# One table of expert slots in device memory, in place of counts and picks in every expert unit

## The chip, the cores and the metric

The kernel runs on one core of a Trainium2 chip. The metric is the time of one execution on the device in microseconds (us), the median of several runs. Engines are named TensorE (PE), VectorE (DVE), ScalarE (ACT), GpSimd (POOL) and SyncE (SP, which issues most transfers).

## The reference

A trunk of two layers over 256 tokens of width 1024, in float32. Layer 0 has neighbourhood attention, attention to a memory and a dense SwiGLU; layer 1 has gated linear attention, attention to the memory and the expert SwiGLU on which the change works:

```
logits = xf @ w_router                                   # 256 tokens, 8 experts
top_val, top_idx = lax.top_k(logits, 2)
weights = softmax(top_val)
y[token] = sum over its two experts e of
           weight * (silu(x @ w_gate[e]) * (x @ w_up[e])) @ w_down[e]
out = rms_norm(h + y)
```

Each expert has three matrices of 1024 x 3584, together 44 MB in float32; the eight experts have 352 MB, which are read once.

## The kernel before, in words

**Units.** The experts run as units of 128 slots: unit 0 to 7 are the experts' first 128 tokens, and up to three further units follow if an expert has more than 128 (with these inputs there are eight units). A unit has 42 weight blocks of 1 MB: for each of seven column blocks c of 512 hidden columns two gate halves, two up halves and two down halves. SyncE loads them some ten blocks ahead. ScalarE writes the rounded high part of a block (`w_hi`, L806), VectorE the rest (`w_lo`, L1399), and TensorE multiplies in three products (`mul3`, L1449: high by high, high by low, low by high). There are three places for cut blocks, so ScalarE may cut a block when TensorE has finished the one three before it.

**Order.** All engines have their program written out by hand; the unit is a loop on each of them (L793 ScalarE, L899 GpSimd, L1389 VectorE, L1944 TensorE), and semaphores tie them. TensorE goes gate(c), turning of the hidden values of c-1, up(c), down(c-1). VectorE cuts low parts in that order, and at the end of each c multiplies the gate's silu by the up product (L1418).

**Which rows a unit takes.** Before the units, VectorE finds the two largest logits of each token (L1313 to 1323) and TensorE sums one-hot masks to each token's rank within its expert (L1924 to 1928). `u_slot` holds for each token and unit the slot, and `u_wt` the weight. For a unit v `build_picks` makes a 0/1 matrix `pick` (token by slot) and puts the weight beside the token's number in `pick_w`:

```python
for t in range(TT):
    dve.tensor_scalar(pick[:, t, :], iota, u_slot[:, t, bass.ds(v, 1)], None,
                      ALU.is_equal).then_inc(pick_ready, 1)
dve.tensor_copy(pick_w[:, :, 1:2], u_wt[:, :, bass.ds(v, 1)]).then_inc(pick_ready, 1)
```

TensorE multiplies `pick` by `pick_w` (`count_picks`, L1985) and so gets, slot by slot, the token's number plus one and its weight. It does so twice in a unit u: behind the products of c = 3 with the picks of u, for the weights and the rows to which the outputs go (`slot_wt`, `row_to`, VectorE at c = 4, L1421 to 1431), and behind c = 5 with the picks of u+1, for the rows to gather (`row_of`, L1433 to 1435). GpSimd then gathers the next unit's rows from `xn_rows` by an indirect transfer (L903), and at a unit's end adds the weighted outputs to `h_rows` by another (L909). Unit 0's rows are not gathered so: TensorE picks them out of `xn` by 32 matmuls (`gather`, L1930).

**What stands ahead of the loop.** VectorE: masks, weights, ranks, picks of unit 0, the list of further units (`unit_i`, L1362 to 1382), the low parts of the gathered rows (`gather_low`, L1384), then the loop. GpSimd: the norm gain (L888), the copies of `xn` and `h` to device memory (L891, L894), then the loop. SyncE at the program's start: constants (L425), router weights (L426), norm gain (L427), then the remaining blocks of the first projection (L429).

Of the kernel before, what the change touches and what calls it, by code (L numbers as in the profile page):

```python
# [129 lines left out]
def shape_constants(np):  # L130

    i = np.arange(P)[:, None]
    j = np.arange(P)[None, :]
    same = (i // CH) == (j // CH)
    col = {}
    parts = []

    def put(name, a):
        full = np.zeros((P, a.shape[1]), np.float32)
        full[: a.shape[0]] = a  # L140
        col[name] = (sum(x.shape[1] for x in parts), a.shape[1])
# [12 lines left out]
    put("iota", np.broadcast_to(np.arange(P), (P, P)))  # L154
    put("token", 1.0 + np.arange(P)[:, None] + P * np.arange(TT)[None, :])
    put("spare", 1.0 + T + np.arange(P)[:, None])
# [16 lines left out]
def build(nc, col, tables, shifts, x, mem, gains, rpb, gate_aug, g_norm, router, mem_kv, even_in, even_out,  # L173
          even_gate, even_up, even_down, odd_in, odd_out, exp_gate, exp_up, exp_down, out):
    with ExitStack() as ctx:
# [29 lines left out]
        pick_w = sb("pick_w", [P, TT, 2])  # L205
        spare_row = sb("spare_row", [P, 1])
# [7 lines left out]
        xn_rows = nc.dram_tensor("xn_rows", (T, D), F32, kind="Internal").ap()  # L214
# [68 lines left out]
        u_slot = take(TT * UCOLS).rearrange("p (t u) -> p t u", t=TT)  # L283
        u_wt = take(TT * UCOLS).rearrange("p (t u) -> p t u", t=TT)
# [43 lines left out]
        r_logit, r_cand, r_one1, r_one2, r_rest, r_mask = (by_expert() for _ in range(6))  # L328
        r_m1, r_m2, r_idx, r_gap, r_gap_exp, r_w1, r_w2 = (take(TT) for _ in range(7))
        r_over, r_number = take(E), take(E)  # L330
# [6 lines left out]
        def STATE_PS(d, k):  # L337
# [47 lines left out]
        pick_ready, slots_counted, slot_part, gathered, gx_hi_ready, gx_lo_ready = (  # L385
            sem("pick_ready"), sem("slots_counted"), sem("slot_part"), sem("gathered"),
            sem("gx_hi_ready"), sem("gx_lo_ready"))
        y_half, y_ready, slot_known, h_kept, pool_turn2 = (
            sem("y_half"), sem("y_ready"), sem("slot_known"), sem("h_kept"), sem("pool_turn2"))
        pool_turn, rows_kept, rows_counted, rows_known, rows_in = (  # L390
            sem("pool_turn"), sem("rows_kept"), sem("rows_counted"), sem("rows_known"), sem("rows_in"))
# [7 lines left out]
        def _(sp):  # L399
# [26 lines left out]
            sp.dma_start(rt_sb[:], router.rearrange(kp, p=P)).then_inc(router_in, 16)  # L426
            sp.dma_start(gnb, g_norm.partition_broadcast(P)).then_inc(gnorm_in, 16)  # L427
# [422 lines left out]
        def _(pool):  # L850
# [38 lines left out]
            for t in range(TT):  # L889
                pool.wait_ge(xn_gained, 2 * (t + 1))  # L890
                nc.gpsimd.dma_start(xn_rows[P * t:P * (t + 1), :], xn[:, t, :]).then_inc(rows_kept, 16)  # L891
# [4 lines left out]
            nc.gpsimd.memset(mhalf[:, 5:6], 0.0).then_inc(pool_turn2, 1)  # L896
            pool.wait_ge(units_ready, 1)
            n_more = pool.value_load(unit_i[0:1, 0:1], min_val=0, max_val=3)
            with pool.Fori(0, n_more + E) as u:  # L899
                pool.wait_ge(rows_known, u + 1)  # L900
                pool.tensor_tensor(mhalf[:, 4:5], mhalf[:, 0:1], mhalf[:, 1:2], ALU.add).then_inc(pool_turn, 1)  # L901
                pool.wait_ge(rows_kept, 16 * TT)
# [12 lines left out]
        def _(dve):  # L915
# [408 lines left out]
            mark(dve.memset(u_slot, -1.0))  # L1324
            mark(dve.memset(u_wt, 0.0))
# [3 lines left out]
            mark(dve.reciprocal(r_w1, r_w1))  # L1329
            settle()  # L1330
            mark(dve.tensor_tensor(r_w2, r_gap_exp, r_w1, ALU.mult))
            settle()
            mark(dve.tensor_tensor(r_one1, r_one1, over_e(r_w1), ALU.mult))
            mark(dve.tensor_tensor(r_one2, r_one2, over_e(r_w2), ALU.mult))
            settle()
            mark(dve.tensor_tensor(u_wt[:, :, 0:E], r_one1, r_one2, ALU.add))
# [6 lines left out]
            mark(dve.tensor_scalar(u_slot[:, :, 0:E], r_cand, -1.0, None, ALU.add))  # L1343
            def build_picks(v):

                for t in range(TT):
                    dve.tensor_scalar(pick[:, t, :], iota, u_slot[:, t, bass.ds(v, 1)], None,
                                      ALU.is_equal).then_inc(pick_ready, 1)
                dve.tensor_copy(pick_w[:, :, 1:2], u_wt[:, :, bass.ds(v, 1)]).then_inc(pick_ready, 1)
# [7 lines left out]

            mark(dve.tensor_copy(pick_w[:, :, 0:1], const("token").unsqueeze(2)))
            settle()
            build_picks(0)  # L1360
# [22 lines left out]

            for b in range(2):  # L1384
                gather_low(0, b)
            dve.memset(ss[:, TT * 5:TT * 6, :], 0.0).then_inc(y_ready, 1)
            dve.wait_ge(units_ready, 1)
            n_more = dve.value_load(unit_i[0:1, 0:1], min_val=0, max_val=3)
            with dve.Fori(0, n_more + E) as u:  # L1389
# [20 lines left out]
                for c in range(NC):  # L1410
# [37 lines left out]
        def _(pe):  # L1448
# [481 lines left out]
            def gather(v, b):  # L1930
                pe.wait_ge(pick_ready, v * 3 + 2)
# [7 lines left out]
            for b in range(2):  # L1939
                gather(0, b)  # L1940
# [3 lines left out]
            with pe.Fori(0, n_more + E) as u:  # L1944
# [40 lines left out]
                def count_picks(at, ready, counted):  # L1985
                    pe.wait_ge(pick_ready, ready)
                    for t in range(TT):
                        ins = pe.matmul(ps[:, 7, at:at + 2], pick[:, t, :], pick_w[:, t, :],
                                        start=(t == 0), stop=(t == 1))
                    ins.then_inc(counted, 1)  # L1990

# [12 lines left out]
                for c in range(NC):  # L2004
# [61 lines left out]
```

## Time and profile before

| | |
|---|---|
| median of 3 runs | 1474.02 us (1472.86 to 1474.33) |
| span of the profiled execution | 1473.3 us (the profile shows no other time for it) |
| PE busy | 1418.6 us, 96% |
| PEld (weight loads) busy | 1188.8 us, 81% |
| DVE busy | 1157.7 us, 79% |
| ACT busy | 1000.6 us, 68% |
| POOL busy | 74.3 us, 5% |
| mean granted clock of TensorE | 0.989 of full speed |
| moved by transfers | 439.40 MB, mean 298 GB/s |

The profile is one execution. Busy shares are averages over all stages; the expert units fill the time from about 494 us to 1454 us. Matmuls are pipelined, so that the listed duration of one overlaps the next, and the distance from start to start is its pace. In a row of a timeline stand the start in us, the duration in us, engine, line, operation, what it writes and reads, and in brackets the idle time before it and what ended it.

### The profile page before, as it was taken

How to read it: one execution, taken by the hardware profiler on the slowest of the kernel's cores; microseconds unless marked ns; L12 is line 12 of the kernel's file. 1: busy time of each engine (PE TensorE's matmuls, PEld its weight loads, DVE VectorE, ACT ScalarE, POOL GpSimd, SP SyncE). 2: the span in 40 equal slices, each digit the busy share in tenths (PEclk: the TensorE clock that was granted, in tenths of full speed). 3: DMA queues.
4: the chain of work that ended last, by engine and by line, in shares of the span. 5: the costliest groups of instructions: out<-in, count | busy, mean ns of one | idle time of the engine just before them, and what ended most of it. 6: DMA issues, size and time to landing. Idle time of an engine off the chain costs nothing.

```text
span 1473.3 us, 19906 instructions
## 1 busy us (share of the span) xinstructions
PE 1418.6 (96%) x7273; PEld 1188.8 (81%) x7273; DVE 1157.7 (79%) x1040; ACT 1000.6 (68%) x949; POOL 74.3 (5%) x72
## 2 busy tenths in 40 slices
PE   6999999998998999999999999999999999999994
PEld 6996888887976788888888888888888888888883
DVE  5677655554674788898888888888889888888885
ACT  6455644445844577877787787787787778778775
POOL 0000000000011100100100100100010010010011
PEclk9999999999999899999999999999999999999997
DMA  9434465544445699999999999999999999999983
GB/s 314 167 115 143 147 203 194 183 135 130 157 158 198 221 380 357 358 404 374 371 379 388 361 374 397 357 367 404 368 347 404 373 369 383 387 359 376 397 304 128
DMA packets 201503, 439.40 MB, mean 298 GB/s; under 512 B 9135, under 2 KB 39411, under 8 KB 201460
## 3 DMA queue, kind: packets, MB, share of 16 engines
q1 hardware_dynamic: 198436, 427.82, 79.4%
q0 software_dynamic: 3024, 11.01, 2.9%
q8 instruction: 27, 0.44, 0.1%
q14 instruction: 16, 0.13, 0.0%
HBM read 430.93 MB, written 7.86 MB: 298 GB/s over the span
## 4 chain that ended last, share of the span: by engine, by line
issue 63%; PE 27%; POOL 3%; DVE 3%; ACT 2%; DMA 1%; POOLq 0%; SPq 0%; DVEq 0%; ACTq 0%
PE ps L1719 6%; PE ps L1451 5%; PE ps L1453 5%; PE ps L1452 5%; PE ps L1721 3%; POOL mhalf L901 1%; POOL arena L903 1%; POOL h_rows L909 1%; DVE w_lo L933 1%; ACT w_hi L516 1%; DMA raw<-mem_kv 1%; PE ps L1472 0%; PE ps L1575 0%; PE ps L1539 0%; PE ps L1902 0%
## 5 line engine op out<-in xcount | busy, mean ns | idle before, releaser
L1399 DVE TENSOR_TENSOR w_lo<-raw,w_hi 128x2048 fp32r<-128x2048 f32 (+1 forms) x224 | 442.2, 1986 | 67.0 <-ACT w_hi L806 65.4
L806 ACT ACTIVATE w_hi<-raw 128x2048 fp32r<-128x2048 f32 (+1 forms) x224 | 372.2, 1672 | 117.4 <-PE ps L1453 117.3
L1451 PE MATMUL ps<-w_hi,xt_both 128*128 128x512 f32 (+2 forms) x1048 | 408.8, 390 | 2.2 <-DVE xt_both L1284 1.5
L1453 PE MATMUL ps<-w_hi,xt_both 128*128 128x512 f32 (+2 forms) x1048 | 400.2, 382 | 0.0
L1452 PE MATMUL ps<-w_lo,xt_both 128*128 128x512 f32 (+2 forms) x1048 | 399.7, 381 | 0.0
L1399 DVE TENSOR_TENSOR w_lo<-arena,w_hi 128x2048 fp32r<-128x2048 f32 x144 | 294.1, 2052 | 20.4 <-ACT w_hi L806 19.7
L806 ACT ACTIVATE w_hi<-arena 128x2048 fp32r<-128x2048 f32 x144 | 248.9, 1728 | 77.1 <-PE ps L1453 77.1
L1451 PEld LDWEIGHTS ps<-w_hi,xt_both 128*128 128x128 f32 x1048 | 197.1, 188 | 44.6 <-DVE w_lo L1399 6.7
L1453 PEld LDWEIGHTS ps<-w_hi,xt_both 128*128 128x128 f32 x1048 | 196.9, 188 | 37.6
L1452 PEld LDWEIGHTS ps<-w_lo,xt_both 128*128 128x128 f32 x1048 | 197.3, 188 | 33.6
L1451 PE MATMUL ps<-w_hi,hT_hi 128*128 128x512 f32 x560 | 219.0, 391 | 0.0
L1453 PE MATMUL ps<-w_hi,hT_lo 128*128 128x512 f32 x560 | 218.3, 390 | 0.0
L1452 PE MATMUL ps<-w_lo,hT_hi 128*128 128x512 f32 x560 | 218.0, 389 | 0.0
L933 DVE TENSOR_TENSOR w_lo<-raw,w_hi 128x2048 fp32r<-128x2048 f32 (+2 forms) x69 | 149.4, 2171 | 68.6 <-ACT w_hi L516 68.5
L516 ACT ACTIVATE w_hi<-raw 128x2048 fp32r<-128x2048 f32 (+2 forms) x70 | 127.1, 1819 | 44.6 <-PE ps L1453 43.5
L1719 PE MATMUL ps<-xt_both,w_hi 128*128 128x512 f32 x352 | 124.9, 399 | 1.0 <-DVE xt_both L974 1.0
L1453 PEld LDWEIGHTS ps<-w_hi,hT_lo 128*128 128x128 f32 x560 | 105.1, 188 | 22.2
L1451 PEld LDWEIGHTS ps<-w_hi,hT_hi 128*128 128x128 f32 x560 | 105.2, 188 | 21.6
L1452 PEld LDWEIGHTS ps<-w_lo,hT_hi 128*128 128x128 f32 x560 | 105.2, 188 | 21.3
L1721 PE MATMUL ps<-xt_both,w_lo 128*128 128x256 f32 x352 | 98.8, 281 | 0.0
L1719 PEld LDWEIGHTS ps<-xt_both,w_hi 128*128 128x128 f32 x352 | 66.1, 188 | 17.7 <-issue 1.2
L1721 PEld LDWEIGHTS ps<-xt_both,w_lo 128*128 128x128 f32 x352 | 66.5, 189 | 0.4
(248 smaller groups left out, 1265.7 us busy)
## 6 DMA issues: line engine op xcount, KB each, us to landing
raw<-exp_gate SPq DMA_DIRECT2D x74, 1024.0 KB, 7.4
raw<-exp_up SPq DMA_DIRECT2D x49, 1024.0 KB, 7.5
arena<-exp_down SPq DMA_DIRECT2D x48, 1024.0 KB, 6.5
arena<-exp_up SPq DMA_DIRECT2D x40, 1024.0 KB, 8.0
raw<-exp_down SPq DMA_DIRECT2D x40, 1024.0 KB, 6.8
arena<-exp_gate SPq DMA_DIRECT2D x24, 1024.0 KB, 6.8
raw<-exp_up SPq DMA_DIRECT2D x32, 512.0 KB, 5.0
raw<-even_gate SPq DMA_DIRECT2D x11, 1024.0 KB, 5.4
```

The source lines that it names most:

```text
L516: act.activation(w_hi[:, n % CUT, 0:w], raw[:, n % RAW, 0:w], ACT.Copy).then_inc(hi_ready, 1)
L806: ins = act.activation(w_hi[:, n % CUT, at:at + src.shape[1]], src, ACT.Copy)
L901: pool.tensor_tensor(mhalf[:, 4:5], mhalf[:, 0:1], mhalf[:, 1:2], ALU.add).then_inc(pool_turn, 1)
L903: nc.gpsimd.indirect_dma_start(gx_rows, None, xn_rows[:, :], bass.IndirectOffsetOnAxis(ap=row_of[:, 0:1], axis=0)).then_inc(rows_in, 16)
L909: nc.gpsimd.indirect_dma_start(h_rows[:, :], bass.IndirectOffsetOnAxis(ap=row_to[:, 0:1], axis=0), y_rows, None, compute_op=ALU.add).then_ ...
L933: dve.tensor_tensor(w_lo[:, n % CUT, 0:w], raw[:, n % RAW, 0:w], w_hi[:, n % CUT, 0:w].bitcast(F32), ALU.subtract).then_inc(lo_ready, 1)
L1399: ins = dve.tensor_tensor(w_lo[:, n % CUT, cols], src, w_hi[:, n % CUT, cols].bitcast(F32), ALU.subtract)
L1451: pe.matmul(dst, a[0], b[0], start=start, stop=False, skip_group_check=shared)
L1452: pe.matmul(dst, a[0], b[1], start=False, stop=False, skip_group_check=shared)
L1453: return pe.matmul(dst, a[1], b[0], start=False, stop=stop, skip_group_check=shared)
L1719: pe.matmul(dst, whi, xt_both[:, k], start=(k == 0), stop=False, skip_group_check=True)
L1721: ins = pe.matmul(dst[:, T:2 * T], wlo, xt_hi[:, k], start=False, stop=(k == KD - 1), skip_group_check=True)
```

## The change

The slots get a table in device memory, 12 columns of 128 slots with two words each: a row number (an integer) and a weight. SyncE fills it at the start with the row numbers 256 to 383 (spare rows) and weight 0. VectorE works out for each token and each of its two experts the place of its slot in the table, and GpSimd writes pairs of row number and weight there by four indirect transfers, and reads the whole table back into `slot_table`, with slots on partitions. In a unit VectorE only copies a column of it. The counts on TensorE and the picks of units 1 and later are gone; unit 0 still takes its rows by picks. Empty slots now gather spare rows, and `xn_rows` has 128 more rows for that.

```diff
+        slot_table = sb("slot_table", [P, UCOLS, 2])
+        slots = nc.dram_tensor("slots", (UCOLS * P, 2), F32, kind="Internal").ap()
+        slots_by_unit = slots.rearrange("(u p) w -> p u w", p=P)
...
SyncE, behind the router weights:
+            sp.dma_start(slots_by_unit, tables[:, at_unused:at_unused + 2 * UCOLS].rearrange("p (u w) -> p u w", w=2)
+                         ).then_inc(slots_cleared, 16)
+            sp.dma_start(slot_pair[:].rearrange("p j t w -> p (j t w)"), tables[:, at_ids:at_ids + 4 * TT]
+                         ).then_inc(row_ids_in, 16)
...
GpSimd, ahead of its loop:
-            for t in range(TT):
-                pool.wait_ge(xn_gained, 2 * (t + 1))
-                nc.gpsimd.dma_start(xn_rows[P * t:P * (t + 1), :], xn[:, t, :]).then_inc(rows_kept, 16)
+            for b in range(TT + 1):
+                pool.wait_ge(xn_gained, 2 * (b % TT + 1))
+                nc.gpsimd.dma_start(xn_rows[P * b:P * (b + 1), :], xn[:, b % TT, :]).then_inc(rows_kept, 16)
...
+            pool.wait_ge(slots_cleared, 16)
+            pool.wait_ge(slots_ready, 2)
+            for j in range(2):
+                for t in range(TT):
+                    nc.gpsimd.indirect_dma_start(
+                        slots[:, :], bass.IndirectOffsetOnAxis(ap=slot_of[:, j, t:t + 1], axis=0),
+                        slot_pair[:, j, t, :], None).then_inc(slots_kept, 16)
+            pool.wait_ge(slots_kept, 16 * 2 * TT)
+            nc.gpsimd.dma_start(slot_table[:], slots_by_unit).then_inc(slots_in, 16)
...
VectorE, ahead of the picks:
-            mark(dve.memset(u_slot, -1.0))
-            mark(dve.memset(u_wt, 0.0))
...
-            mark(dve.tensor_tensor(r_w2, r_gap_exp, r_w1, ALU.mult))
-            settle()
-            mark(dve.tensor_tensor(r_one1, r_one1, over_e(r_w1), ALU.mult))
-            mark(dve.tensor_tensor(r_one2, r_one2, over_e(r_w2), ALU.mult))
-            settle()
-            mark(dve.tensor_tensor(u_wt[:, :, 0:E], r_one1, r_one2, ALU.add))
+            dve.tensor_tensor(slot_pair[:, 1, :, 1], r_gap_exp, slot_pair[:, 0, :, 1], ALU.mult).then_inc(slots_ready, 1)
...
-            mark(dve.tensor_copy(pick_w[:, :, 0:1], const("token").unsqueeze(2)))
-            settle()
-            build_picks(0)
...
VectorE, the list of further units:
-            for dst, vals, off in ([(unit_f[:, 1:4], i8, 0.0)]
-                                   + [(u_slot[:, t, E:E + 3], u_slot[:, t, 0:E], -float(P)) for t in range(TT)]
-                                   + [(u_wt[:, t, E:E + 3], u_wt[:, t, 0:E], 0.0) for t in range(TT)]):
-                mark(dve.tensor_tensor(r_prod, r_sel, vals.unsqueeze(1).broadcast_to([P, 3, E]), ALU.mult))
-                settle()
-                mark(dve.tensor_reduce(r_sum, r_prod, AX_X, ALU.add))
-                settle()
-                mark(dve.tensor_scalar(dst, r_sum, off, None, ALU.add))
-                settle()
+            mark(dve.tensor_tensor(r_prod, r_sel, i8.unsqueeze(1).broadcast_to([P, 3, E]), ALU.mult))
...
+            mark(dve.tensor_reduce(unit_f[:, 1:4], r_prod, AX_X, ALU.add))
...
VectorE, behind gather_low of unit 0 and ahead of its loop:
+            mark(dve.tensor_tensor(r_shift, r_number, i8, ALU.subtract))
+            mark(dve.tensor_scalar(r_past, u_slot, float(P) - 0.5, None, ALU.is_gt))
+            mark(dve.scalar_tensor_tensor(r_place, over_t(i8), float(P), u_slot, ALU.mult, ALU.add))
+            settle()
+            mark(dve.tensor_scalar(r_shift, r_shift, float(E - 2), float(P), ALU.add, ALU.mult))
+            settle()
+            mark(dve.tensor_tensor(r_past, r_past, over_t(r_shift), ALU.mult))
+            settle()
+            mark(dve.tensor_tensor(r_place, r_place, r_past, ALU.add))
+            settle()
+            mark(dve.tensor_tensor(r_prods, r_one, r_place.unsqueeze(1).broadcast_to([P, 2, TT, E]), ALU.mult))
+            settle()
+            mark(dve.tensor_reduce(r_slot, r_prods, AX_X, ALU.add))
+            settle()
+            dve.tensor_copy(slot_of[:], r_slot).then_inc(slots_ready, 1)
...
VectorE, in a unit:
-                        dve.wait_ge(slots_counted, u + 1)
-                        row = ps[:, 7, 0:1]
-                        dve.scalar_tensor_tensor(spare_row[:], row, 0.0, const("spare"), ALU.is_equal, ALU.mult
-                                                 ).then_inc(slot_part, 1)
-                        dve.tensor_copy(slot_wt[:], ps[:, 7, 1:2]).then_inc(slot_known, 1)
-                        dve.wait_ge(slot_part, u + 1)
-                        dve.scalar_tensor_tensor(row_to[:], row, -1.0, spare_row[:], ALU.add, ALU.add
-                                                 ).then_inc(slot_known, 1)
-                        build_picks(u + 1)
+                        dve.wait_ge(slots_in, 16)
+                        dve.tensor_copy(slot_wt[:], slot_table[:, bass.ds(u, 1), 1]).then_inc(slot_known, 1)
+                        dve.tensor_copy(row_to[:], slot_table[:].bitcast(U32)[:, bass.ds(u, 1), 0]).then_inc(slot_known, 1)
                     if c == 5:
-                        dve.wait_ge(rows_counted, u + 1)
                         dve.wait_ge(pool_turn, u + 1)
-                        dve.tensor_scalar(row_of[:], ps[:, 7, 2:3], -1.0, 0.0, ALU.add, ALU.max).then_inc(rows_known, 1)
+                        dve.tensor_copy(row_of[:], slot_table[:].bitcast(U32)[:, bass.ds(u + 1, 1), 0]
+                                        ).then_inc(rows_known, 1)
...
TensorE, in a unit:
-                    if c == 3:
-                        count_picks(0, u * 3 + 3, slots_counted)
-                    if c == 5:
-                        count_picks(2, u * 3 + 6, rows_counted)
```

## Rows read from the trace of the kernel before

**Rows 1.** Busy in the second unit: stretch, its length, PE, PEld, DVE, ACT, POOL, clock.
```profile
615.00:735.00 120.00, 120.00 (x551) 98.93 (x550) 106.42 (x74) 92.81 (x72) 6.44 (x4) 1.00 1.02 378
```

**Rows 2.** Waits, 500 to 1450 us: who for whom, us in total, times, longest.
```profile
ACT w_hi L806 <- PE ps L1453: 205.7, 288, 1.3
...
PEld ps L1451 <- DVE w_lo L1399: 6.7, 23, 0.5
```

**Rows 3.** Timeline of PE in the second unit, around a count.
```profile
667.68 0.39 PE L1451 MATMUL ps<-w_hi,xt_both 128*128 128x512 f32 x1
...
675.61 0.40 PE L1453 MATMUL ps<-w_hi,hT_lo 128*128 128x512 f32 x1
675.84 0.51 PE L1988 MATMUL ps<-pick_w,arena 128*128 128x2 f32 x4
...
676.53 0.40 PE L1452 MATMUL ps<-w_lo,xt_both 128*128 128x512 f32 x1
```

**Rows 4.** Timeline: DVE at c = 4 of unit 0; PE behind it in unit 1.
```profile
572.56 0.15 DVE L1425 SCALAR_TENSOR_TENSOR spare_row<-ps,cst 128x1 f32<-128x1 f32 x1
...
573.63 4.49 DVE L1399 TENSOR_TENSOR w_lo<-arena,w_hi 128x2048 fp32r<-128x2048 f32 x2 [0.19 <-issue]
...
695.82 0.47 PE L1451 MATMUL ps<-w_hi,xt_both 128*128 128x512 f32 x1
696.13 0.39 PE L1452 MATMUL ps<-w_lo,xt_both 128*128 128x512 f32 x1
```

**Rows 5.** Timeline of PE and DVE, 488 to 500 us.
```profile
488.82 5.41 PE L1934 MATMUL ps<-arena,xn 128*128 128x128 f32 x32 [0.30 <-DVE pick_w L1349]
489.06 0.32 DVE L1368 SCALAR_TENSOR_TENSOR arena<-arena 128x8 f32<-128x8 f32 x3
489.42 0.18 DVE L1374 TENSOR_TENSOR arena<-arena,cst 128x24 f32<-128x24 f32 x1
489.64 0.18 DVE L1376 TENSOR_REDUCE arena<-arena 128x3 f32<-128x24 f32 x1
...
494.18 0.49 PE L1451 MATMUL ps<-w_hi,xt_both 128*128 128x512 f32 x1
...
494.90 0.69 DVE L1353 TENSOR_TENSOR xt_both<-ps,xt_both 128x512 fp32r<-128x512 f32 x1 [1.10 <-ACT xt_both L785]
...
496.03 2.29 DVE L1399 TENSOR_TENSOR w_lo<-raw,w_hi 128x2048 fp32r<-128x2048 f32 x1 [0.43 <-issue]
...
499.75 0.39 PE L1451 MATMUL ps<-w_hi,xt_both 128*128 128x512 f32 x1
```

**Rows 6.** Instructions on the tile `unit_i`: duration in ns, first and last start.
```profile
L1388 DVEq TENSOR_LOAD <-unit_i x1: 549/549/549, 494.9 to 494.9; - x1
```

**Rows 7.** Instructions on the tensor `h_rows`: duration in ns, first and last start.
```profile
L909 POOL DMA_INDIRECT h_rows<-arena,row_to x8: 1596/1600/1634, 616.2 to 1455.2; - x8
L894 POOL DMA_DIRECT2D h_rows<-h x3: 533/533/533, 482.0 to 483.1; - x3
```

**Rows 8.** Transfers: issued by, count, KB each, median us from issue to landing.
```profile
cst<-tables SPq DMA_DIRECT2D x1, 385.5 KB, 10.1
h_rows<-arena,row_to POOLq DMA_INDIRECT x8, 10.2
...
states<-router SPq DMA_DIRECT2D x1, 32.0 KB, 10.7
```

**Rows 9.** Timeline of SyncE's queue at the start.
```profile
16.16 0.98 SPq L425 DMA_DIRECT2D cst<-tables  x1
17.18 0.44 SPq L426 DMA_DIRECT2D states<-router  x1
17.66 4.25 SPq L427 DMA_DIRECT2D gain<-g_norm  x1
```

**Rows 10.** Timeline of ACT at the start.
```profile
32.07 1.92 ACT L516 ACTIVATE w_hi<-raw 128x2048 fp32r<-128x2048 f32 x1
...
44.59 0.60 ACT L601 ACTIVATE arena<-ps 128x512 f32<-128x512 f32 x1 [5.34 <-PE ps L1453]
```

More of the change, by code:

```diff
@@ L154, in shape_constants @@
     put("iota", np.broadcast_to(np.arange(P), (P, P)))
-    put("token", 1.0 + np.arange(P)[:, None] + P * np.arange(TT)[None, :])
-    put("spare", 1.0 + T + np.arange(P)[:, None])
+    spare = np.stack([T + np.arange(P), np.zeros(P)], 1).astype(np.uint32)
+    put("unused", np.tile(spare, (1, UCOLS)).view(np.float32))
+    rows = np.zeros((P, 2, TT, 2), np.uint32)
+    rows[..., 0] = np.arange(P)[:, None, None] + P * np.arange(TT)
+    put("row_ids", rows.reshape(P, 4 * TT).view(np.float32))
     x, dc = np.arange(SHIFT_W)[None, :], np.arange(RPB_C)[:, None]
@@ L204, in build @@
         gnb = gain[:, 0:DV]
-        pick_w = sb("pick_w", [P, TT, 2])
-        spare_row = sb("spare_row", [P, 1])
+        slot_pair = sb("slot_pair", [P, 2, TT, 2])
+        slot_of = sb("slot_of", [P, 2, TT], U32)
+        slot_table = sb("slot_table", [P, UCOLS, 2])
+        slots = nc.dram_tensor("slots", (UCOLS * P, 2), F32, kind="Internal").ap()
+        slots_by_unit = slots.rearrange("(u p) w -> p u w", p=P)
         row_to = sb("row_to", [P, 1], U32)
@@ L213, in build @@
         row_of = sb("row_of", [P, 1], U32)
-        xn_rows = nc.dram_tensor("xn_rows", (T, D), F32, kind="Internal").ap()
+        xn_rows = nc.dram_tensor("xn_rows", (T + P, D), F32, kind="Internal").ap()
         states = sb("states", [P, 2, 3, DV])
@@ L282, in build @@
         pick = take(TT * P).rearrange("p (t s) -> p t s", t=TT)
-        u_slot = take(TT * UCOLS).rearrange("p (t u) -> p t u", t=TT)
-        u_wt = take(TT * UCOLS).rearrange("p (t u) -> p t u", t=TT)
+        u_slot = take(TT * E).rearrange("p (t e) -> p t e", t=TT)
         unit_f = take(4)
@@ L326, in by_expert @@
             return take(TT * E).rearrange("p (t e) -> p t e", t=TT)
-        r_logit, r_cand, r_one1, r_one2, r_rest, r_mask = (by_expert() for _ in range(6))
-        r_m1, r_m2, r_idx, r_gap, r_gap_exp, r_w1, r_w2 = (take(TT) for _ in range(7))
-        r_over, r_number = take(E), take(E)
+        r_logit, r_cand, r_rest, r_mask, r_past, r_place = (by_expert() for _ in range(6))
+        r_one = take(2 * TT * E).rearrange("p (j t e) -> p j t e", j=2, t=TT)
+        r_one1, r_one2 = r_one[:, 0], r_one[:, 1]
+        r_prods = take(2 * TT * E).rearrange("p (j t e) -> p j t e", j=2, t=TT)
+        r_slot = take(2 * TT).rearrange("p (j t) -> p j t", j=2)
+        r_m1, r_m2, r_idx, r_gap, r_gap_exp, r_w1 = (take(TT) for _ in range(6))
+        r_over, r_number, r_shift = take(E), take(E), take(E)
         r_sel = take(3 * E).rearrange("p (j e) -> p j e", j=3)
@@ L384, in build @@
             sem("silu_ready"), sem("hid_ready"), sem("hid_turned"), sem("hT_hi_ready"), sem("hT_lo_ready"))
-        pick_ready, slots_counted, slot_part, gathered, gx_hi_ready, gx_lo_ready = (
-            sem("pick_ready"), sem("slots_counted"), sem("slot_part"), sem("gathered"),
-            sem("gx_hi_ready"), sem("gx_lo_ready"))
+        pick_ready, gathered, gx_hi_ready, gx_lo_ready = (
+            sem("pick_ready"), sem("gathered"), sem("gx_hi_ready"), sem("gx_lo_ready"))
+        slots_cleared, row_ids_in, slots_ready, slots_kept, slots_in = (
+            sem("slots_cleared"), sem("row_ids_in"), sem("slots_ready"), sem("slots_kept"), sem("slots_in"))
         y_half, y_ready, slot_known, h_kept, pool_turn2 = (
             sem("y_half"), sem("y_ready"), sem("slot_known"), sem("h_kept"), sem("pool_turn2"))
-        pool_turn, rows_kept, rows_counted, rows_known, rows_in = (
-            sem("pool_turn"), sem("rows_kept"), sem("rows_counted"), sem("rows_known"), sem("rows_in"))
+        pool_turn, rows_kept, rows_known, rows_in = (
+            sem("pool_turn"), sem("rows_kept"), sem("rows_known"), sem("rows_in"))
         h_back = [sem(f"h_back_{t}") for t in range(TT)]
@@ L901, in _ @@
                 pool.tensor_tensor(mhalf[:, 4:5], mhalf[:, 0:1], mhalf[:, 1:2], ALU.add).then_inc(pool_turn, 1)
-                pool.wait_ge(rows_kept, 16 * TT)
+                pool.wait_ge(rows_kept, 16 * (TT + 1))
                 nc.gpsimd.indirect_dma_start(gx_rows, None, xn_rows[:, :],
@@ L1328, in _ @@
             settle()
-            mark(dve.reciprocal(r_w1, r_w1))
+            dve.wait_ge(row_ids_in, 16)
+            mark(dve.reciprocal(slot_pair[:, 0, :, 1], r_w1))
             settle()
-            mark(dve.tensor_tensor(r_w2, r_gap_exp, r_w1, ALU.mult))
-            settle()
-            mark(dve.tensor_tensor(r_one1, r_one1, over_e(r_w1), ALU.mult))
-            mark(dve.tensor_tensor(r_one2, r_one2, over_e(r_w2), ALU.mult))
-            settle()
-            mark(dve.tensor_tensor(u_wt[:, :, 0:E], r_one1, r_one2, ALU.add))
+            dve.tensor_tensor(slot_pair[:, 1, :, 1], r_gap_exp, slot_pair[:, 0, :, 1], ALU.mult).then_inc(slots_ready, 1)
             dve.wait_ge(ranks_done, 1)
@@ L1342, in _ @@
             settle()
[L1343 to L1349, printed above, removed]
+            mark(dve.tensor_scalar(u_slot, r_cand, -1.0, None, ALU.add))
+            settle()
+            for t in range(TT):
+                dve.tensor_scalar(pick[:, t, :], iota, u_slot[:, t, 0:1], None, ALU.is_equal).then_inc(pick_ready, 1)
             def gather_low(v, b):
@@ L1385, in _ @@
                 gather_low(0, b)
+            mark(dve.tensor_tensor(r_shift, r_number, i8, ALU.subtract))
[9 more added lines that the diff above has]
+            mark(dve.tensor_tensor(r_prods, r_one, r_place.unsqueeze(1).broadcast_to([P, 2, TT, E]), ALU.mult))
+            settle()
+            mark(dve.tensor_reduce(r_slot, r_prods, AX_X, ALU.add))
+            settle()
+            dve.tensor_copy(slot_of[:], r_slot).then_inc(slots_ready, 1)
             dve.memset(ss[:, TT * 5:TT * 6, :], 0.0).then_inc(y_ready, 1)
@@ L1928, in _, with gather @@
                 pe.matmul(dst, second, r_mask[:, 1, :], start=False, stop=True).then_inc(ranks_done, 1)
-            def gather(v, b):
-                pe.wait_ge(pick_ready, v * 3 + 2)
+            def gather(b):
+                pe.wait_ge(pick_ready, 2)
                 for k in range(4 * b, 4 * b + 4):
@@ L1939, in _ @@
             for b in range(2):
-                gather(0, b)
+                gather(b)
             pe.wait_ge(units_ready, 1)
@@ L1983, in down @@
                         ins.then_inc(slot_done, 1)
[L1985 to L1990, printed above, removed]
                 def turn_rows(u, b):
```

1 line of the change is left out of this document (added).

## The prediction

> **What bounds the kernel now.** I read the stretches of the eight expert units first. In the second of them TensorE is busy 120.00 of 120 us at full granted clock, VectorE 106.4, ScalarE 92.8 [rows 1]. A busy TensorE need not be a TensorE at its pace, so the waits of that stage come next: ScalarE stands 205.7 us before its cut of a weight block, in 288 waits, always for TensorE; TensorE's weight loads wait for VectorE's low part only 6.7 us in total, and no wait on a transfer is among the listed rows [rows 2]. So the transfers are ahead, the two cutting engines follow TensorE, and time falls only where TensorE issues less or stutters less. The start times show its pace: from 667.68 to 675.61 us there are 35 steps, 7.93 us, so 0.2266 us from one 512-column matmul to the next [rows 3].
>
> **What the change takes from a unit.** (a) The two counts. Each is four matmuls of 2 columns between two runs of wide ones. Around one of them the last wide matmul before it starts at 675.61 and the second one after it at 676.53: 0.92 us, where two steps of 0.2266 would be 0.45 [rows 3]. That is 0.47 us for one count. There are two in a unit (behind blocks c = 3 and c = 5) and eight units (the scatter of a unit's outputs has eight rows [rows 7]), so 16 x 0.47 = 7.5 us. All of it lies on TensorE, which has nothing beside it: the whole sum counts.
>
> (b) VectorE's work at c = 4. Before, it makes the spare row, the weight, the row number, two picks and a weight copy between 572.56 us and the next weight cut at 573.63: 1.07 us [rows 4]. Two copies stay; one such copy or one-column operation takes about 0.15 us [rows 4], so some 0.7 us of it goes. What is late because of it: the low part of the second gate block of c = 5. There TensorE's step from 695.82 to 696.13 is 0.31 instead of 0.227 us [rows 4], 0.08 us too much. With 0.7 us returned VectorE is in time, so I take 8 x 0.08 = 0.6 us; the ends are 0 and twice that. VectorE's wait for the second count, ahead of the row numbers at c = 5, goes as well; I give it nothing, because the low parts behind it arrive in time today.
>
> **Could the 7.5 us come back as a wait?** After a block TensorE frees a place, ScalarE cuts it, VectorE subtracts, and TensorE needs it two blocks later. ScalarE's waits for TensorE average 205.7 / 288 = 0.7 us per block [rows 2]: that chain has about this much to spare at every block, and it is paced by TensorE's own block ends, so it moves forward with them. Two blocks with a count inside now get the time that all the others already have. I count no return; it is the first rival below.
>
> **What the change does ahead of the units.** VectorE's chain from the masks to the unit list loses most of its length: five groups of product, sum and offset at about 0.21 us a step (489.42 to 489.64 [rows 5]) become one. That is worth nothing: behind the picks TensorE gathers the first rows from 488.82 on for 5.4 us, up to the first unit matmul at 494.18 [rows 5], and the list is ready before that. Only what stands in front of the picks counts; one copy of the token numbers goes and one wait is added there, which makes the gather some 0.07 us earlier. I take 0.1 us gained.
>
> The slot arithmetic comes back later in VectorE's order, behind the second low part of the gathered rows and ahead of the loop, and there it is in the way. That low part starts at 494.90 and ends at 495.59; today the loop's first cut starts at 496.03, ends at 498.32 (2.29 us), and TensorE wants this third block at 499.75 [rows 5]. VectorE's register load of the unit count starts at 494.9, on release of the last wait [rows 6], and the cut follows 1.13 us behind it. The new chain: three independent operations, 0.36 us like the three at 489.06 [rows 5]; then five dependent ones (shift, its product, the sum, the two products with the one-hot masks, the reduction) at 0.21 us = 1.05. The last wait is released at 495.59 + 1.41 = 497.00, the cut starts at 498.13 and ends at 500.42. TensorE would want it at 499.75, so it stands 0.67 us, once; the fourth block, cut by 502.7, is wanted by 503.1 and is in time. I take 0.7 us lost. The ends are 0, if the register load overlaps the chain, and 1.4, if the steps are twice as long.
>
> **The table itself.** GpSimd gets four small scatters and one read back ahead of its loop. It idles until the first unit's row numbers at 590 us, and VectorE first needs the table at c = 4 of unit 0, at 572.56 [rows 4]. One indirect transfer holds GpSimd 1.6 us and lands after 10.2 us; a plain one of 128 rows holds it 0.53 us [rows 7, 8]. From 497.2: 4 x 1.6 + 10.2 = 513.8. The read back has 1536 pieces of 8 bytes; at the indirect rate, 12.5 ns a piece, it takes 19.2 us to issue, and lands at 543.2, about 29 us before it is needed. Even at 34 ns a piece (below) it is there at about 576, 4 us late. I cost it at nothing; the ends are 0 and 4 us lost. The extra 0.5 MB of spare rows falls into a stretch in which transfers are far ahead. The rows of empty slots now come from 128 different places and no longer all from row 0: as many bytes, hidden behind two blocks of the unit.
>
> At the start SyncE clears the table: 1536 pieces of 8 bytes, queued between the router weights and the norm gains, ahead of the third and later weight blocks. The nearest row is the router transfer, 1024 pieces of 32 bytes: issued at 17.18, landed 10.7 us later, at 27.9, where the table of constants ahead of it landed at 16.16 + 10.1 = 26.3 [rows 8, 9]. So 1024 pieces took at most 1.6 us, and 1536 take 2.4. The other end is the norm gain: 128 pieces held SyncE 4.25 us [rows 9], 34 ns a piece, which for 1536 would be 52 us. The cover: ScalarE cuts the next weight block at 32.07 without waiting for its transfer, and first needs to be free again at 44.59, when TensorE's output of the first block is done [rows 10]. With 1.9 us for the cut, 10.6 us of delay cost nothing. I take 2.4 us, hidden; the router row is the nearer one, since its pieces are as many and as small, and SyncE held only 0.44 us for them.
>
> The Trainium skill speaks against this edit: "DMA: Bandwidth & Descriptors", sections "Rules for kernel authors" and "Measured", says that a last dimension that is not contiguous becomes one descriptor per element, and puts a packet at about 10.5 ns. By that the clearing would take some 16 us, an estimate from that page, and the sum would end 5.5 us higher, near 1472; the router row, 1.6 ns a piece, does not bear the page's figure out for pieces spread over all engines.
>
> **The sum.** 7.5 + 0.6 + 0.1 - 0.7 = 7.5 us gained. The profiled execution's span is 1473.3 us, its own time is not shown beside that; the span is 0.7 us below the median of the runs, 1474.02, so I take the gain off the median: 1466.5 us, and a span near 1465.8.
>
> **Rivals.**
> First, the counts are free room: their 0.47 us is time in which the cutting chain catches up, and without them TensorE waits for low parts at c = 4 and c = 6. For it: that chain has only 0.7 us to spare per block. Against it: five of seven blocks c have no count, and TensorE keeps 0.2266 us through them [rows 3]. Then only the loop's late start is left: 1474.0 + 0.7 - 0.1 = 1474.6.
>
> Second, on the slower side: the clearing transfer blocks SyncE. Its place is SyncE's queue at 17.6 us. Its price is up to 34 ns a piece, 52 us, of which 10.6 are covered; it begins to cost at 7 ns a piece and outweighs the gain from 12 ns. For it: the norm gain's 4.25 us for 128 pieces. Against it: the router's 1024 pieces. At the full price it ends at 1466.5 + 41 = 1508.
>
> Third, the same price in part: the pieces are slow but not that slow, and the delay of about 16 us eats 5.5 us of the gain: 1472, no measurable change. The page named above would have it so.
>
> **How the numbers follow.** Forecast 0.86; counts are free room 0.04; clearing at a middle price 0.05; clearing at a full price 0.05. About 0.2%, 3 us, is what a measurement of this kernel can tell from no change: so faster 0.86 (the forecast), same 0.09 (the two between), slower 0.05. The forecast's own range: the counts 7.0 to 7.7, the stutter at c = 5 0 to 1.2, the loop start 0 to 1.4 lost, the read back up to 4 lost, which is less likely, and some 0.8 us of scatter between runs: 1464.5 to 1469.5. That holds about 8 in 10 of all cases.
>
> **What would show it.** Right: no 2-column matmuls in the units, 0.2266 us from the last wide matmul of c = 3's down product to the first of c = 4's gate; units of about 118.8 us instead of 119.9; one stop of TensorE of half a us or so in front of the third block of unit 0; GpSimd's read back landed long before c = 4. Wrong: waits of TensorE for low parts that were not there, a late third weight block near 32 us, a wait of VectorE at c = 4 of unit 0, or units as long as before.

## The result and the profile after

The changed kernel takes 1466.29 us (median; 1464.75 to 1466.8) against 1474.17 us of the kernel before in the same comparison: ratio 0.9937, 95% interval 0.9926 to 0.9949. The profiled execution has a span of 1465.0 us, 8.3 us shorter than before, at a mean granted clock of 0.988. In a later comparison (its unedited run stands below) it took 1466.77 us, ratio 0.9943 (0.993 to 0.9956).

First the length of a unit. VectorE copies the next unit's rows (`row_of`) at c = 5 of each unit, so first and last start of that instruction are seven units apart. Instructions on the tile `row_of` (duration in ns, first and last start), before:

```profile
L1435 DVE TENSOR_SCALAR row_of<-ps x8: 157/158/159, 590.7 to 1429.7; 128x1 uint32<-128x1 f32 x8
```

and after:

```profile
L1449 DVE COPY row_of<-slot_table x8: 146/149/150, 589.5 to 1421.2; 128x1 uint32 x8
```

That is 839.0 / 7 = 119.86 us before and 831.7 / 7 = 118.81 after: 1.05 us a unit, 8.4 us over eight. One by one the seven distances are 119.82 to 119.88 us before and 118.79 to 118.88 after. So the gain lies in the units, spread evenly over them.

Busy times in the second unit after the change (stretch, its length, PE, PEld, DVE, ACT, POOL, clock), against [rows 1]:

```profile
615.00:735.00 120.00, 120.00 (x547) 99.04 (x546) 105.86 (x70) 93.85 (x71) 6.65 (x6) 1.00 1.03 380
```

Nothing is to be seen in it: TensorE was full and is full. A busy share cannot show a gain of 0.9% that comes from work left out on an engine that is busy before and after.

The waits after the change, 500 to 1450 us (us in total, times, longest), against [rows 2]:

```profile
ACT w_hi L821 <- PE ps L1468: 198.7, 290, 0.9
...
PEld ps L1466 <- DVE w_lo L1420: 5.4, 15, 1.1
...
PE ps L1466 <- DVE w_lo L1420: 0.7, 1, 0.7
```

ScalarE still waits for TensorE at most blocks (290 waits, 288 before), and the waits of TensorE's weight loads for low parts became fewer (15 and not 23). No count came back as a wait. The one wait of 0.7 us is new; it is at the loop's start (below).

TensorE's timeline where the first count stood, after the change (start, duration, engine, line, operation); [rows 3] has the same place with the count:

```profile
674.70 0.39 PE L1467 MATMUL ps<-w_lo,hT_hi 128*128 128x512 f32 x1
674.93 0.39 PE L1468 MATMUL ps<-w_hi,hT_lo 128*128 128x512 f32 x1
675.16 0.39 PE L1466 MATMUL ps<-w_hi,xt_both 128*128 128x512 f32 x1
675.38 0.39 PE L1467 MATMUL ps<-w_lo,xt_both 128*128 128x512 f32 x1
```

Between the down product of one block and the gate of the next the steps are 0.23, 0.23 and 0.22 us: the ordinary pace.

VectorE at c = 4 of the second unit, after (the first row is the product of the gate's silu and the up product, called the hidden product here):

```profile
690.87 0.68 DVE L1439 TENSOR_TENSOR arena<-arena,ps 128x512 f32<-128x512 f32 x1
...
691.59 2.28 DVE L1420 TENSOR_TENSOR w_lo<-arena,w_hi 128x2048 fp32r<-128x2048 f32 x1
```

The low part starts 0.72 us behind the start of the hidden product. TensorE at the block that needs it, the second gate block of c = 5:

```profile
694.67 0.39 PE L1466 MATMUL ps<-w_hi,xt_both 128*128 128x512 f32 x1
694.90 0.39 PE L1467 MATMUL ps<-w_lo,xt_both 128*128 128x512 f32 x1
```

The step of 0.31 us that [rows 4] shows there is gone: it is 0.23 us.

The table ahead of the loop and GpSimd's part, timeline of GpSimd, after (in brackets idle time and what ended it):

```profile
497.94 1.07 POOL L916 DMA_INDIRECT slots<-slot_pair,slot_of  x1 [13.85 <-DVE slot_of L1406]
...
503.70 1.89 POOL L916 DMA_INDIRECT slots<-slot_pair,slot_of  x1 [0.30 <-issue]
511.60 1.09 POOL L920 DMA_DIRECT2D slot_table<-slots  x1 [6.01 <-DMA slots<-slot_pair,slot_of]
```

and the transfers (issued by, count, KB each, median us to landing):

```profile
slots<-slot_pair,slot_of POOLq DMA_INDIRECT x4, 7.2
...
slot_table<-slots POOLq DMA_DIRECT2D x1, 12.0 KB, 6.8
```

The table is in at 511.6 + 6.8 = 518.4 us; VectorE reads it first at 572.7. That leaves 54 us to spare.

The loop's start, VectorE after, against [rows 5]:

```profile
496.93 0.17 DVE L1406 CAST slot_of<-arena 128x4 uint32<-128x4 f32 x1
...
498.06 4.50 DVE L1420 TENSOR_TENSOR w_lo<-raw,w_hi 128x2048 fp32r<-128x2048 f32 x2 [0.96 <-issue]
```

and TensorE:

```profile
499.34 0.39 PE L1468 MATMUL ps<-w_hi,xt_both 128*128 128x512 f32 x1
500.41 0.50 PE L1466 MATMUL ps<-w_hi,xt_both 128*128 128x512 f32 x1 [0.69 <-DVE w_lo L1420]
```

This is a step of 1.07 us where 0.23 is usual: 0.84 us lost, once.

The program's start, SyncE's queue after, against [rows 9]:

```profile
16.88 0.44 SPq L436 DMA_DIRECT2D states<-router  x1
17.36 4.35 SPq L438 DMA_DIRECT2D slots<-tables  x1
21.75 5.20 SPq L440 DMA_DIRECT2D slot_pair<-tables  x1
26.98 1.64 SPq L442 DMA_DIRECT2D gain<-g_norm  x1
28.66 19.27 SPq L414 DMA_DIRECT2D raw<-even_in  x8
```

and ScalarE, against [rows 10]:

```profile
36.59 1.91 ACT L531 ACTIVATE w_hi<-raw 128x2048 fp32r<-128x2048 f32 x1 [4.35 <-DMA raw<-even_in]
39.30 1.92 ACT L531 ACTIVATE w_hi<-raw 128x2048 fp32r<-128x2048 f32 x1 [0.80 <-DMA raw<-even_in]
44.64 0.60 ACT L616 ACTIVATE arena<-ps 128x512 f32<-128x512 f32 x1 [3.42 <-PE ps L1468]
```

SyncE stands 11.2 us at three small transfers, where it stood 4.25 at one. The weight cut of 32.07 comes at 36.59, 4.5 us later, and now waits for its transfer. Yet ScalarE copies TensorE's first output at 44.64 and copied it at 44.59: the delay is swallowed. A second cut (39.30) stands between the first one and that copy, and behind it ScalarE still waits 3.42 us for TensorE. These 3.42 us are what is left of the cover, the delay that costs nothing.

### The profile page after: what moved, and what is told of

The parts are those of the page before. It is cut to its first block, busy times and chain, and to the rows that moved or that the text cites. A ratio compares the mean times of both kernels' runs of the same rounds, so it can differ in the third digit from the quotient of the medians.

```text
span 1465.0 us, 19721 instructions
## 1 busy us (share of the span) xinstructions
PE 1410.5 (96%) x7209; PEld 1182.9 (81%) x7209; DVE 1150.8 (79%) x997; ACT 1000.5 (68%) x949; POOL 75.8 (5%) x78
## 4 chain that ended last, share of the span: by engine, by line
issue 63%; PE 28%; POOL 3%; DVE 3%; ACT 2%; DMA 1%; POOLq 0%; SPq 0%; DVEq 0%; ACTq 0%
PE ps L1734 6%; PE ps L1466 5%; PE ps L1467 5%; PE ps L1468 5%; PE ps L1736 3%; POOL mhalf L925 1%; POOL h_rows L933 1%; DVE w_lo L957 1%; ACT w_hi L531 1%; POOL arena L927 1%; DMA raw<-mem_kv 1%; PE ps L1487 0%; PE ps L1590 0%; POOL slots L916 0%; PE ps L1917 0%
```

## The experiments

Theory A: the gain is TensorE's time for the small matmuls, some 0.47 us a count, and nothing else of size. Rivals: the counts are free room and something else shortens the units (the shorter work of VectorE at c = 4 above all); or a count's price is the break in the row of wide matmuls, not its own matmuls. Beside it stand the two places where the change lost or might have lost: the loop's start, and the clearing at the program's start. The first four runs share a chip (kernel before: 1475.62 us), the last four another (1475.21 us).

**Counts put back on TensorE alone.** The matmuls stand where they stood and nobody reads their result; the table stays.

```diff
+                def count_picks(at):
+                    for t in range(2):
+                        pe.matmul(ps[:, 7, at:at + 2], pick[:, t, :], const("ones")[:, 0:2],
+                                  start=(t == 0), stop=(t == 1))
...
+                    if c == 3:
+                        count_picks(0)
+                    if c == 5:
+                        count_picks(2)
```

> The changed kernel with the counts put back on TensorE alone: behind c = 3 and c = 5 of every unit four matmuls of 2 columns (in the program two, one for each half of the tokens) into a bank that nobody reads. VectorE's work stays as in the changed kernel. Theory (TensorE issues less): 16 x 0.47 = 7.5 us come back, 1473.8 us, units of 119.8 us. Rival 1 (VectorE was relieved: about 0.7 us of work and a wait of 0.9 us less in each unit): the counts alone cost little, 1466.3 to 1467.5. Rival 2 (the counts stood in free room): no change, 1466.3.

Measured: 1474.52 us, ratio to the kernel before 1.0004 (0.9995 to 1.0013). The gain is gone, as far as can be told: the medians are 1.1 us apart, and the interval holds 1. TensorE around the count:

```profile
674.89 0.40 PE L1468 MATMUL ps<-w_hi,hT_lo 128*128 128x512 f32 x1
675.12 0.50 PE L2002 MATMUL ps<-cst,arena 128*128 128x2 f32 x4
675.49 0.48 PE L1466 MATMUL ps<-w_hi,xt_both 128*128 128x512 f32 x1
675.80 0.39 PE L1467 MATMUL ps<-w_lo,xt_both 128*128 128x512 f32 x1
```

From 674.89 to 675.80 there are 0.91 us in place of two steps, as in [rows 3]. The units' length:

```profile
L1449 DVE COPY row_of<-slot_table x8: 144/145/148, 588.9 to 1427.5; 128x1 uint32 x8
```

838.6 / 7 = 119.80 us, so two counts cost 0.99 us a unit and the rest of the change is worth 0.06 there. This is the main evidence: theory A holds, and counts as free room are ruled out.

**Half of each count.** One of its two matmuls (two recorded of four).

```diff
-                    for t in range(2):
+                    for t in range(1):
                         pe.matmul(ps[:, 7, at:at + 2], pick[:, t, :], const("ones")[:, 0:2],
-                                  start=(t == 0), stop=(t == 1))
+                                  start=(t == 0), stop=(t == 0))
```

> As the run before, but each count covers only one half of the tokens, so half as many small matmuls and weight loads. If the price of a count is the break in the stream of wide matmuls, nearly all of it stays: 1473 us. If it is the weight loads that no wide matmul hides, about half of it is left: 0.2 to 0.28 us for one, 3.5 to 4.5 us in all, 1469.8 to 1470.8.

Measured: 1472.11 us, ratio 0.998 (0.9971 to 0.9989). That lies between the two expectations, 1.3 us above the range for half the price and 0.9 below the figure for the break, so the time alone does not decide. TensorE:

```profile
676.36 0.40 PE L1468 MATMUL ps<-w_hi,hT_lo 128*128 128x512 f32 x1
676.59 0.28 PE L2002 MATMUL ps<-cst,arena 128*128 128x2 f32 x2
676.73 0.47 PE L1466 MATMUL ps<-w_hi,xt_both 128*128 128x512 f32 x1
677.05 0.40 PE L1467 MATMUL ps<-w_lo,xt_both 128*128 128x512 f32 x1
```

0.69 us from 676.36 to 677.05, so 0.24 for the half count where the whole one takes 0.46. The units are (1426.1 - 590.6) / 7 = 119.36 us long, 0.55 more than after the change, where the whole counts add 0.99. So the trace decides: a count costs by its matmuls, and a fixed price for the break comes out at 0.02 us a count by the start times and 0.055 by the units. Whether the small matmuls themselves or the weight loads ahead of them take the time is not separated by these runs.

**VectorE's work put back, without counts.** At c = 4 two one-column operations, two comparisons of 128x128 and a copy, with results that nobody reads.

```diff
...
+                        for n in range(2):
+                            (dve.scalar_tensor_tensor(spare[:, n:n + 1], iota[:, 0:1], 0.0, iota[:, 1:2],
+                                                          ALU.is_equal, ALU.mult))
+                        for t in range(TT):
+                            dve.tensor_scalar(pick[:, t, :], iota, slot_table[:, bass.ds(u + 1, 1), 1], None,
+                                              ALU.is_equal)
+                        dve.tensor_copy(spare[:, 2:4], iota[:, 0:2])
```

> The changed kernel with VectorE's old work at c = 4 put back as work without use: two one-column operations, two 128 x 128 comparisons and a small copy, some 0.8 us in each unit; no counts. Theory (VectorE's part is only the stutter at c = 5): 0.08 us a unit and somewhat more in unit 0 come back, 1466.9 to 1467.2 us. Rival (VectorE's relief is what made the units shorter): 0.8 us a unit come back, 1472.7.

Measured: 1467.3 us, ratio 0.9955 (0.9941 to 0.9969): the gain stays, and VectorE's relief as its cause falls. The step at c = 5 that the expectation wanted back did not come back: TensorE's step at the second gate block is 0.22 us (694.61 to 694.83). VectorE:

```profile
690.81 0.68 DVE L1440 TENSOR_TENSOR arena<-arena,ps 128x512 f32<-128x512 f32 x1
...
692.13 4.49 DVE L1421 TENSOR_TENSOR w_lo<-arena,w_hi 128x2048 fp32r<-128x2048 f32 x2
```

Its low part starts 1.32 us behind the start of the hidden product. The kernel before, at the same place:

```profile
692.02 0.68 DVE L1418 TENSOR_TENSOR arena<-arena,ps 128x512 f32<-128x512 f32 x1
...
693.44 4.50 DVE L1399 TENSOR_TENSOR w_lo<-arena,w_hi 128x2048 fp32r<-128x2048 f32 x2
```

That distance is 1.42, with the long step; after the change it is 0.72, without. TensorE comes to the block 3.80 us behind the start of the hidden product in all three, so the distances compare, and the border lies between 1.32 and 1.42 us. In this unit the kernel before was over it by at most 0.1, and almost any cut of VectorE's work there would have done. In unit 0, where the distance is 1.67 us (571.96 to 573.63), it was over by a quarter of a microsecond more, and TensorE's two steps at the block (575.54 to 576.31) are together 0.3 us too long.

**The slots' arithmetic earlier.** The block of VectorE's operations from `r_shift` to `slot_of` stands ahead of the two low parts of the gathered rows, and no longer behind them.

```diff
-            for b in range(2):
-                gather_low(0, b)
             mark(dve.tensor_tensor(r_shift, r_number, i8, ALU.subtract))
...
             dve.tensor_copy(slot_of[:], r_slot).then_inc(slots_ready, 1)
+            for b in range(2):
+                gather_low(0, b)
```

> The changed kernel with VectorE's slot arithmetic moved ahead of the low parts of the gathered rows, into the time in which it stands there (3.2 us). Theory (the late loop start costs TensorE one stop of 0.7 us in front of the third block of unit 0): the stop goes, 1465.5 us, and the table is ready 5 us sooner. Rival (the stop is taken up later by the cutting chain): no change, 1466.3.

Measured: 1467.02 us, ratio 0.995 (0.9936 to 0.9964). The stop is gone: VectorE starts the third block's cut at 496.75 and TensorE goes through its first step at 500.24 without a pause. But TensorE came there no earlier:

```profile
488.29 6.66 PE L1949 MATMUL ps<-arena,xn 128*128 128x128 f32 x32 [0.23 <-DVE arena L1364]
494.70 0.48 PE L1466 MATMUL ps<-w_hi,xt_both 128*128 128x512 f32 x1
```

The 32 matmuls ahead of the loop took 6.66 us, and 5.65 in the profiled execution of the changed kernel. A table by stretches of this run (length, PE, PEld, DVE, ACT, POOL, clock) says why:

```profile
490.00:492.00 2.00, 2.00 (x11) 2.00 (x11) 0.88 (x5) 0.00 (x0) 0.15 (x1) 0.50 0.35 129
492.00:494.00 2.00, 2.00 (x12) 2.00 (x11) 0.69 (x1) 0.60 (x1) 1.70 (x2) 0.50 0.01 1
```

The granted clock is 0.50 (1.2 GHz) until 494, where the changed kernel's row for 492 to 494 has 0.89. From the first unit matmul (494.70) to the first turning of unit 0 (511.33) it is 16.63 us here, and 17.44 in the changed kernel (493.99 to 511.43). The lost 0.8 us is thus shown to be the arithmetic's place; that removing it shortens the kernel is not.

**Four clears in place of one.** Three more of the same transfer, into tensors that nothing reads.

```diff
+        more_slots = [nc.dram_tensor(f"more_slots_{n}", (UCOLS * P, 2), F32, kind="Internal").ap()
+                      .rearrange("(u p) w -> p u w", p=P) for n in range(3)]
...
+            for more in more_slots:
+                sp.dma_start(more, tables[:, at_unused:at_unused + 2 * UCOLS].rearrange("p (u w) -> p u w", w=2)
+                             ).then_inc(more_cleared, 16)
```

> Three more clears of the same 1536 pieces of 8 bytes follow the first one in SyncE's queue, into three other tensors that nothing reads. Cover theory (one clear costs nothing because the second block of even_in has room before TensorE wants it): the first clear held SyncE for 4.35 us, so three more hold it some 13 us; the next cut comes at about 49.6 us instead of 36.59, the low part of that block about 54.8 instead of 41.7, and TensorE wants the block at 45.92. TensorE then stops for about 9 us near 46 us and the kernel takes 1473 to 1476 us. Rival A (a clear holds the queue only for its issue, 0.5 us, and the 4.35 us were the other transfers in flight): cut at most 2 us later, 1466 to 1467 us. Rival B (the price of 1536 pieces is paid in full, at the 34 ns a piece of the gains' broadcast): three times 52 us of queue, kernel above 1550 us.

Measured: 1477.65 us, ratio 1.0018 (1.001 to 1.0027), 10.9 us above the changed kernel on that chip: more than expected. SyncE:

```profile
17.10 4.34 SPq L441 DMA_DIRECT2D slots<-tables  x1
21.49 10.50 SPq L444 DMA_DIRECT2D more_slots<-tables  x3
```

ScalarE behind it:

```profile
46.34 1.91 ACT L537 ACTIVATE w_hi<-raw 128x2048 fp32r<-128x2048 f32 x1 [14.92 <-DMA raw<-even_in]
49.49 1.91 ACT L537 ACTIVATE w_hi<-raw 128x2048 fp32r<-128x2048 f32 x1 [1.24 <-DMA raw<-even_in]
51.30 0.58 ACT L622 ACTIVATE arena<-ps 128x512 f32<-128x512 f32 x1
```

and TensorE, which waits for the copy that ScalarE makes behind the second of these cuts:

```profile
43.76 1.51 PE L1596 MATMUL ps<-hT_lo,hT_hi 128*128 128x72 f32 x12
51.94 0.58 PE L1472 MATMUL ps<-xt_both,w_hi 128*128 128x256 f32 x1 [6.67 <-ACT arena L622]
52.31 0.42 PE L1473 MATMUL ps<-xt_both,w_hi 128*128 128x256 f32 x1
...
56.37 0.31 PE L1474 MATMUL ps<-xt_both,w_lo 128*128 128x256 f32 x1
```

The three clears hold SyncE 10.5 us, 3.5 each, and the cut comes at 46.34 instead of 36.59: 9.75 us, 3.25 for each clear. TensorE then stands 6.67 us. Behind the stop its granted clock is 0.50 (1.2 GHz) in the stretch from 53 to 56, and the 19 steps from 52.31 to 56.37 take 0.214 us each instead of 0.12: 1.8 us more. The first row reduction that follows (VectorE) starts 8.0 us later than in the changed kernel, 62.5 against 54.5, and the gather 9.9 us later (498.49 against 488.58); where the last 1.9 of these come from was not separated. The expectation put the stop at some 9 us, more than it was, and still came out too low, since it left out the clock. What it was to tell apart it tells: one clear stays within the cover of that block, four do not.

**The clear and the pairs' load late.** Both transfers are issued behind the odd projection's weights, long before they are needed.

```diff
-            sp.dma_start(slots_by_unit, tables[:, at_unused:at_unused + 2 * UCOLS].rearrange("p (u w) -> p u w", w=2)
...
             for c in range(2):
                 halves(S_OUT1 + 2 * c, odd_out, 512 * c, 512)
+            sp.dma_start(slots_by_unit, tables[:, at_unused:at_unused + 2 * UCOLS].rearrange("p (u w) -> p u w", w=2)
...
```

> The clear and the load of the table's pairs are issued by SyncE behind the odd projection's weights instead of ahead of the first blocks of even_in. Cover theory: the next cut goes back from 36.59 to about 32 us, and the time stays within 0.5 us of the changed kernel's, since TensorE never waited for it: 1465.5 to 1467. Rival (the 4.5 us later cut did cost something by a way that the profile does not show): 2 us or more faster than the changed kernel, under 1464.5.

The changed kernel ran beside it, unedited, as the measure of that chip:

> The changed kernel itself, as the measure for the other runs on this chip. Both theories (the counts paid for the gain; or the counts were free room and the gain came from elsewhere) expect what it gave when its result came: 1466.3 us, 1464.7 to 1467.3, ratio to the kernel before 0.993 to 0.9955.

Measured: 1465.76 us, ratio 0.994 (0.9927 to 0.9954), for the edit, and 1466.77 us, 0.9943 (0.993 to 0.9956), for the changed kernel. The cut is back at 31.52 us:

```profile
31.52 1.92 ACT L531 ACTIVATE w_hi<-raw 128x2048 fp32r<-128x2048 f32 x1
```

The medians are 1.0 us apart, and each kernel's own runs spread over 2 us or more, so the time is the same within what can be told. That is what the cover theory expects. A cost of a microsecond is not ruled out by the times; the trace of the changed kernel shows none, since ScalarE waits for TensorE behind the late cuts.

**Late loads and early arithmetic together.** Both edits at once, as the best version that the runs suggested.

> As the run before this one, and the slots' arithmetic ahead of the low parts of unit 0's second pair of gathers (as in e3_slots_earlier). The prediction's term of 0.7 us for a late loop start says 0.7 us faster than the changed kernel if nothing takes its place: 1465.6. Rival (what e3's trace showed: the stop before the third block goes, but unit 0's small stops at 508 us come back and the gather's own length depends on the granted clock at that point): no difference that can be measured, 1466 to 1467.

Measured: 1465.95 us, ratio 0.9944 (0.9931 to 0.9957). The stop at the third block is gone, and the first turning of unit 0 comes 16.65 us behind the first unit matmul (492.73 to 509.38), where the run before this one needs 17.45 (492.45 to 509.90). A small one of 0.28 us stands at 506.2 instead, as in the kernel before at 507.7. The time does not differ measurably from the changed kernel's. The span of 1463.7 us is 1.3 us shorter; one execution does not show that this is the edits.

## Why the prediction was right

**The counts** were the gain, as the prediction said, and its size holds: 7.5 us from rows, 0.99 x 8 = 7.9 us by the run that put them back. A count, two matmuls of 2 columns in the program and four in the record, costs as much as two wide steps.

**The step at c = 5** went as predicted, 0.6 us in the sum. The units of the kernel before are 0.06 us longer than those with counts and without VectorE's work, 0.4 us over seven; that is no more than the 0.06 by which runs with equal units differ (118.81 to 118.87), but the long step itself stands in the one trace and not in the other. With 0.3 us in unit 0 it makes 0.7. The reason given (0.7 us returned to VectorE) was more than was needed: 0.1 us was enough in the later units.

**The loop's start** was worked out to the tenth: cut at 498.13, TensorE stopped 0.67 us. It was 498.06 and a wait of 0.69, in a step 0.84 too long. Neither of the ends (register load beside the chain; steps twice as long) came.

**The gather 0.1 us earlier** cannot be read off: its start moves more than that from run to run (487.04 to 489.46 among the runs without a delay at the start).

**The table** was costed at nothing, rightly, and its working was far too slow: the read back was put at 543.2 us and landed at 518.4. The step that failed is the rate of an indirect transfer, 12.5 ns a piece, carried to a plain one: its 1536 pieces held GpSimd 1.09 us and landed in 6.8. The packet records of the trace show a difference that the working had no row for: the read back went as 32 packets of 256 or 512 bytes, while the clear, as many pieces in SyncE's queue, went as 1536 packets of 8 bytes.

**The clear** was taken as 2.4 us of queue, hidden, and it was hidden, but the working was wrong in three places. Its price is 3.25 us by the added clears, 2.1 ns a piece in place of the router's 1.6; the first clear's own share of the 4.5 us was not separated. The other small load, `slot_pair`, 128 rows of 32 bytes, got no term: SyncE stands 5.20 us at it, longer than at the clear. And the cover was put at 10.6 us, as if one cut stood ahead of ScalarE's copy at 44.59. The kernel before has two there:

```profile
37.34 1.91 ACT L516 ACTIVATE w_hi<-raw 128x2048 fp32r<-128x2048 f32 x1 [3.35 <-PE ps L1453]
```

Of a cover of some 7.9 us (4.5 used and 3.42 left) the change left 3.4, not the 8.2 of the prediction; that the term came out at nothing is in part luck. The prediction also named a late block near 32 us as a sign of failure; the block was 4.5 us late, and that was no sign of anything, because it stayed within this cover. The upper price is a slip, too: 4.25 us for 128 pieces are 33 ns, not 34, which changes nothing.

The Trainium skill's figure of about 10.5 ns a packet ("DMA: Bandwidth & Descriptors", section "Measured"), which stands there for a transfer issued from GpSimd, would make a clear some 16 us if its packets went one after another, an estimate from that page. The trace bears out the figure and not the sum: the clear's 1536 packets take 17.4 us added up, 11.3 ns each, but all of them lie between 22.74 and 29.09 us, so they ran side by side, and an added clear delays the next load by 3.25 us.

**The rivals.** Free room: ruled out by the counts put back. Clearing at the full or at a middle price: by the prediction's own cover they were to cost something from 7 ns a piece, and the price is 2.1. The mechanism itself is real: with four clears the kernel is slower than before.

**The sum**: 7.5 us predicted, 7.88 measured between the medians; the measured pieces give 7.9 + 0.7 - 0.8 = 7.8. Units of 118.8 us were predicted, and 118.81 measured.

## What to carry to other kernels

On an engine that is busy all the time, price what goes by the distance of start times around it, and multiply. Here small matmuls between wide ones cost far more than their columns, and their cost came back in full because the engines that feed TensorE followed its pace. A delay in a queue cost nothing up to the cover of the next block that was wanted, and beyond it the stop, with TensorE's lower clock on top. So work out the cover first, then the delay, and count into the cover all that the waiting engine has to do before the block is wanted: here a second cut was left out. A piece's price holds for the kind of transfer on which it was read.

## What was not expected of the hardware

- Small transfers hold SyncE for microseconds at this place: 128 rows of 32 bytes 5.20 us, 1536 pieces of 8 bytes 4.35 us, while 1024 pieces of 32 bytes ahead of them held it 0.44 us. The norm gains took 4.25 us before, and 1.64 us behind the two new ones. So it looks like a queue that is full of what stands ahead; that was not tested by itself.
- The same 32 matmuls ahead of the loop took 5.33 to 6.66 us in these runs, by the stretch in which TensorE's granted clock came back to 1.00. An edit of a few tenths there can't be judged by one profile.
- A stop of 6.67 us cost TensorE 1.8 us more behind it, at the granted clock of 0.50 (1.2 GHz).
